# Two pairs of feed-forward units per layer as seven block products, with two of the four weight sums made by accumulating DMA

## What is computed

```
def swiglu(x, w_gate, w_up, w_down):
    return (jax.nn.silu(x @ w_gate) * (x @ w_up)) @ w_down
...
        x = x + 0.5 * swiglu(rms_norm(x, norm_g[i, 0]), ffn_w_gate[i, 0], ffn_w_up[i, 0], ffn_w_down[i, 0])
        h = rms_norm(x, norm_g[i, 1])
...
        x = x + mix @ w_o[i]
        x = x + 0.5 * swiglu(rms_norm(x, norm_g[i, 2]), ffn_w_gate[i, 1], ffn_w_up[i, 1], ffn_w_down[i, 1])
    return rms_norm(x, final_g)
```

## Time and profile before

| | |
|---|---|
| median of 3 runs | 1964.34 us (1964.17 to 1964.35) |
| the profiled execution | 1965.22 us, of it 1963.4 us span |
| PE busy | 1945.8 us (99%), 10556 matmuls |
| DVE busy | 1219.4 us (62%) |
| ACT busy | 949.7 us (48%) |
| POOL busy | 41.1 us (2%) |
| PE's share of the chain that ended last | 97% |
| DMA | 348.80 MB, 178 GB/s on average |
| granted PE clock | 0.996 of full speed |

### The profile page before, as it was taken

The page is one execution under the profiler, slowest core; times in us unless marked ns, Lnnn a source line. Parts: engine busy times, 40 slices in busy tenths (PEclk is TensorE's granted clock), DMA queues, the critical chain, the costliest instruction groups (busy, mean ns, idle before and its releaser), DMA issues.

```text
span 1963.4 us, 26311 instructions
## 1 busy us (share of the span) xinstructions
PE 1945.8 (99%) x10556; PEld 1681.9 (86%) x10556; DVE 1219.4 (62%) x1179; ACT 949.7 (48%) x1018; POOL 41.1 (2%) x34
## 2 busy tenths in 40 slices
PE   9999999999999999999999999999999999999998
PEld 7888998888888898888888889988888888988887
DVE  6555657655755678755575555775557556557554
ACT  5444545444544444644454443454445444545443
POOL 0000000000000000100000000000000000000000
PEclk9999999999999999999999999999999999999999
DMA  7654443555455453555445543445554554535541
GB/s 253 234 188 186 157 152 150 206 186 187 186 186 186 168 193 109 185 199 192 172 177 189 191 152 129 171 169 206 186 188 172 193 192 150 194 128 193 191 187 71
DMA packets 49872, 348.80 MB, mean 178 GB/s; under 512 B 6145, under 2 KB 6401, under 8 KB 7937
## 3 DMA queue, kind: packets, MB, share of 16 engines
q1 hardware_dynamic: 49360, 346.54, 47.9%
q10 hardware_dynamic: 432, 1.11, 0.2%
HBM read 346.58 MB, written 1.05 MB: 177 GB/s over the span
## 4 chain that ended last, share of the span: by engine, by line
PE 97%; DVE 2%; DMA 0%; ACT 0%; issue 0%; POOLq 0%; POOL 0%; DVEq 0%; ACTq 0%
PE work L1202 27%; PE work L1200 12%; PE acc L1071 9%; PE acc L1073 9%; PE acc L1072 9%; PE work L1071 7%; PE work L1073 7%; PE work L1072 7%; PE work L1205 2%; PE acc L1115 1%; PE work L1385 1%; DVE w_lo L629 1%; PE work L1372 1%; PE work L1262 0%; DMA x<-x_dram 0%; PE work L1386 0%
## 5 line engine op out<-in xcount | busy, mean ns | idle before, releaser
L629 DVE TENSOR_TENSOR w_lo<-raw,w_hi 128x2048 fp32r<-128x2048 f32 x327 | 746.7, 2288 | 123.7 <-ACT w_hi L376 121.2
L1202 PE MATMUL work<-xn,w_hi 128*128 128x512 f32 x2304 | 795.6, 393 | 0.0
L376 ACT ACTIVATE w_hi<-raw 128x2048 fp32r<-128x2048 f32 x327 | 620.9, 1908 | 16.0 <-DMA raw<-stream_dram 16.0
L1200 PE MATMUL work<-xn,w_lo 128*128 128x256 f32 x2016 | 567.4, 281 | 0.0
L1202 PEld LDWEIGHTS work<-xn,w_hi 128*128 128x128 f32 x2304 | 417.6, 188 | 75.6
L1200 PEld LDWEIGHTS work<-xn,w_lo 128*128 128x128 f32 x2016 | 379.7, 188 | 13.9
L1071 PE MATMUL acc<-w_hi,m_hi 128*128 128x512 f32 x824 | 325.1, 395 | 1.2 <-DVE m_lo L845 0.6
L1073 PE MATMUL acc<-w_hi,m_lo 128*128 128x512 f32 x824 | 321.2, 390 | 0.0
L1072 PE MATMUL acc<-w_lo,m_hi 128*128 128x512 f32 x824 | 320.8, 389 | 0.0
L435 ACT ACTIVATE scratch<-work 128x512 f32<-128x512 f32 x72 | 43.2, 600 | 431.9 <-PE work L1202 431.9
L726 DVE TENSOR_TENSOR scratch<-work,scratch 128x512 f32<-128x512 f32 x72 | 49.8, 692 | 276.3 <-ACT scratch L435 276.3
(11 more groups left out here) (177 smaller groups left out, 1721.9 us busy)
## 6 DMA issues: line engine op xcount, KB each, us to landing
raw<-stream_dram SPq DMA_DIRECT2D x327, 1024.0 KB, 4.8
x<-x_dram SPq DMA_DIRECT2D x2, 512.0 KB, 7.7
raw<-stream_dram ACTq DMA_DIRECT2D x2, 512.0 KB, 7.4
cst<-consts_dram SPq DMA_DIRECT2D x1, 832.0 KB, 6.8
out_dram<-x SPq DMA_DIRECT2D x3, 256.0 KB, 2.4
final_gain<-final_gain_dram SPq DMA_DIRECT2D x1, 512.0 KB, 7.5
out_dram<-wide SPq DMA_DIRECT2D x1, 256.0 KB, 2.9
cst<-consts_dram ACTq DMA_DIRECT2D x1, 64.0 KB, 1.9
```

The lines of the kernel that those rows point to most:

```text
L376: nc.scalar.activation(w_hi[:, c % RING, :], raw[:, c % RAW, :], ACT.Copy).then_inc(hi_ready, 1)
L629: nc.vector.tensor_tensor(w_lo[:, c % RING, :], raw[:, c % RAW, :], w_hi[:, c % RING, :].bitcast(F32), ALU.subtract).then_inc(lo_ready, 1)
L1200: nc.tensor.matmul(bank[:, 0:T], lo, xn_hi[:, k, :], start=False, stop=False, skip_group_check=True)
L1202: ins = nc.tensor.matmul(halves(bank), hi, xn[:, :, k, :], start=k == 0, stop=k == DT - 1, skip_group_check=True)
```

## The change

In each FFN the units 4 and 5, and the units 8 and 9, become a pair (`SEVEN = 4, 8`). The gate and up product of a pair is a matrix product of two token blocks (128 tokens each) by two halves of the inner dimension, with weights of two halves by two units: four blocks `b11`, `b12`, `b21`, `b22`, each a chunk of 512 inner rows by 512 columns (256 of gate, 256 of up). Eight block products would be needed; here seven are made (`PARTS`), from four sums of weight blocks (`t1` to `t4`) and four sums of token blocks (`S1` to `S4`):

- `t1` is `b11` plus `b12`, `t3` is `b12` plus `b22`: both sums are made by a DMA from POOL's queue that adds a second chunk from HBM onto a chunk in SBUF (`accum_op`). `b11` is loaded twice for that, the second time into a new buffer `extra`. The signs are in how the chunks are combined.
- `t2` is the sum of `t3` and `b11`, `t4` the sum of `b21` and `t2`: two adds on DVE of a whole chunk (`form`, L786 and L789), in place in `raw`, and in `extra`.
- each of the seven chunks is then split as any other; `quarter` makes one block product: 12 matmuls with tokens (or token sums) as stationary operand and 512 weight columns moving.
- the token sums are made once per FFN, in unit 2: four DVE adds, four ACT copies, four DVE subtractions of 512 numbers per partition (`token_sums`, `token_sums_hi`, `token_sums_lo`).
- the seven results are combined in PSUM, by accumulation, and on DVE and ACT (`pair_step`), and the hidden values are transposed on PE (`pair_hidden`: two groups of four transposes), during the gate of the unit after the pair.
- the down product of the unit after the first of a pair moves into the pair; the unit after the pair does two down products. The loops are gone; everything is written out in full. The weights are in the stream as loads (`LOADS`) and as uses (`USES`), which are no longer the same list: 376 uses, 344 loads and 32 adding DMAs, where before there were 328 of each.

The new order of chunks in units 7, 8, 9 and 10 is: top 7, bottom 7, down 6, then `b11`, `t1`, `t2`, `b21`, `t3`, down 7, `t4`, `b22`, then top 10, down 8, bottom 10, down 9, down 10. The diff, cut to its core:

```
+SEVEN = 4, 8
+PLAIN = [s for s in range(UNITS) if s not in SEVEN and s - 1 not in SEVEN]
+OWN = PLAIN[TURNED:]
+HIDDEN = [s for s in range(UNITS) if s not in OWN]
 PAIRS = D // COLS
-FFN_CHUNKS = 3 * UNITS
+FFN_CHUNKS = 3 * UNITS + 3 * len(SEVEN)
...
+def plan():
+    uses, loads, users, places = [], [], [], {}
+    for layer, n, c0, att, no in phases():
+        order = ATT_ORDER if att else FFN_ORDER
+        for w, (what, j) in enumerate(order, c0):
+            p = no * len(SEVEN) + SEVEN.index(j) if what in PARTS else None
+            if what in ("t1", "t4"):
+                uses.append((what, no, j, SUMS, None))
+            elif what == "b22":
+                uses.append((what, no, j, EXTRA, p + 1))
+            elif what in ("t2", "t3"):
+                uses.append((what, no, j, *places["b11" if what == "t2" else "b12"]))
+            else:
+                uses.append((what, no, j, len(users) % RAW, len(users) // RAW + 1))
+            for load in ("b12",) if what == "t1" else () if what in FORMS or what in ("t3", "b22") else (what,):
+                r = len(users)
+                places[load] = r % RAW, r // RAW + 1
+                loads.append((load, layer, n % 3, j, r % RAW, users[r - RAW] if r >= RAW else None))
+                users.append(("form", len(FORMS) * (p + 1)) if load in ("b11", "b21") else
+                             ("lo", c0 + order.index(("t3", j)) + 1) if load == "b12" else ("lo", w + 1))
+            if what == "t1":
+                earlier = SEVEN.index(j) - 1
+                loads.insert(-1, ("b11", layer, n % 3, j, SUMS,
+                              ("gu", (no * len(PLAIN) + TURNED) * TB) if earlier < 0 else
+                              ("lo", c0 + order.index(("t4", SEVEN[earlier])) + 1)))
+                loads.append(("b22", layer, n % 3, j, EXTRA,
+                              ("gu", (no * len(PLAIN) + TURNED) * TB) if earlier < 0 else
+                              ("lo", c0 + order.index(("b22", SEVEN[earlier])) + 1)))
+    return uses, loads
...
-                sp.dma_start(raw[:, c % RAW, :], stream[chunk]).then_inc(raw_loaded[c % RAW], 16)
+            def load(i):
+                place, free = LOADS[i][4:]
+                if free is not None:
+                    sp.wait_ge({"lo": lo_ready, "form": form_ready, "gu": gu_psum}[free[0]], free[1])
...
+
+                for i, j in enumerate(SEVEN):
+                    p = f * len(SEVEN) + i
...
+                    pool.wait_ge(sums_loaded, 16 * (p + 1))
+                    pool.dma_start(raw_at(SUMS), stream[b12], accum_op=ALU.add).then_inc(t1_ready, 16)
+                    pool.wait_ge(raw_loaded[place], 16 * loads_of_b12)
+                    pool.dma_start(raw_at(place), stream[b22], accum_op=ALU.add).then_inc(t3_ready, 16)
...
+                def own_step_of(s):
...
+                    if not after:
+                        split_to(g + 3)
+                    if s == TURNED:
+                        hidden_hi(s - 1, unit_bank(s - 1, 0))
+                    if ahead and not after:
+                        split_to(g + 5)
+                    act.wait_ge(top_used, plain + 1)
+                    nc.scalar.activation(gate_rest, own_bank(0)[:, :, T:2 * T], ACT.Copy).then_inc(gate_rest_ready, 1)
+                    split_to(g + (3 if after else 6 if ahead else 4))
+                    act.wait_ge(gate_ready, own_u + 1)
+                    nc.scalar.activation(gate_sb, gate_sb, ACT.Silu).then_inc(own_silu_ready, 1)
...
+                    if after:
+                        split_to(g + 6)
+                    act.wait_ge(gu_psum, plain * TB + 2)
+                    nc.scalar.activation(up_rest, own_bank(1)[:, :, T:2 * T], ACT.Copy).then_inc(up_rest_ready, 1)
+                    if not after:
+                        split_to(g + (7 if ahead else 5))
+                    act.wait_ge(own_h_ready, own_u + 1)
+                    nc.scalar.activation(m_hi[:, u % 2 * 2:u % 2 * 2 + 2, :], up_sb, ACT.Copy).then_inc(h_hi_ready, 1)
+                    if after:
+                        split_to(g + 7)
...
+                def pair_step(s):
...
+
+                    split_to(q + 5)
+                    copied(1, 0, first_part)
+                    split_to(q + 6)
...
+            def form(what, q):
+
+                no, j = USES[q][1:3]
+                p = no * len(SEVEN) + SEVEN.index(j)
+                place = {part: USES[q + PAIR_ORDER.index(part)][3] for part in PAIR_ORDER}
+                b11, b12, b21, b22 = (raw_at(place[part]) for part in ("t2", "t3", "b21", "b22"))
+                if what == "t2":
+                    dve.wait_ge(t3_ready, 16 * (p + 1))
+                    ins = nc.vector.tensor_tensor(b11, b12, b11, ALU.add)
+                else:
+                    dve.wait_ge(form_ready, len(FORMS) * p + 1)
+                    ins = nc.vector.tensor_tensor(raw_at(SUMS), b21, b11, ALU.add)
+                ins.then_inc(form_ready, 1)
 
...
+                def own_step_of(s):
...
+                    if not after:
+                        split_to(g + 3)
+                    if s == TURNED:
+                        hidden_lo(s - 1, unit_bank(s - 1, 0))
+                        token_sums()
+                    if ahead:
+                        split_to(g + 4)
+                        form("t2", g + 3)
+                        split_to(g + 5)
+                    dve.wait_ge(gate_rest_ready, own_u + 1)
                     nc.vector.tensor_tensor(gate_sb, own_bank(0)[:, :, 0:T], gate_rest, ALU.add).then_inc(gate_ready, 1)
-                    split_next(1)
-                    dve.wait_ge(up_rest_ready, own_u + 1 + turn * 2)
+                    split_to(g + (6 if after or ahead else 4))
+                    if ahead:
+                        form("t4", g + 3)
+                    dve.wait_ge(up_rest_ready, own_u + 1)
                     nc.vector.tensor_tensor(up_sb, own_bank(1)[:, :, 0:T], up_rest, ALU.add).then_inc(up_ready, 1)
-                    dve.wait_ge(own_silu_ready, own_u + 1 + turn * 2)
...
+                def quarter(bank, part, c, first, last):
+                    pe.wait_ge(lo_ready, c + 1)
+                    for k in range(FIRST_KS):
+                        a_hi, a_lo = part(k)
+                        ins = product(work[:, bank, :], a_hi, a_lo, wide_chunk(w_hi, c)[:, k, :], wide_chunk(w_lo, c)[:, k, :],
+                                      start=first and k == 0, stop=last and k == FIRST_KS - 1, skip=True)
+                    ins.then_inc(part_psum, 1)
+
+                def pair_step(s):
+                    p, q, own_u = f * len(SEVEN) + SEVEN.index(s), c0 + FFN_ORDER.index(("b11", s)), f * len(OWN) + OWN.index(s - 1)
+                    block_of = lambda tb, half: lambda k: tuple(
+                        w[:, half * FIRST_KS + k, tb * P:(tb + 1) * P] for w in (xn_hi, xn_lo))
+                    sum_of = lambda i: lambda k: token_part(i, k)
+                    pe.wait_ge(gate_ready, own_u + 1)
+                    quarter(0, block_of(0, 0), q, True, False)
+                    pe.wait_ge(up_ready, own_u + 1)
+                    if s == SEVEN[0]:
+                        pe.wait_ge(token_lo_ready, BANKS * (f + 1))
+                    quarter(3, sum_of(S1), q + 1, True, False)
+                    quarter(1, sum_of(S2), q + 2, True, False)
+                    pe.wait_ge(part_copied, 2 * p + 1)
+                    quarter(0, block_of(0, 1), q + 3, False, True)
+                    pe.wait_ge(pair_sums_ready, 5 * p + 1)
+                    quarter(1, sum_of(S3), q + 4, False, False)
+                    unit_down(s - 1).then_inc(down_used, 1)
+                    pe.wait_ge(pair_sums_ready, 5 * p + 2)
+                    quarter(1, block_of(1, 1), q + 6, False, True)
+                    pe.wait_ge(part_copied, 2 * p + 2)
+                    quarter(3, sum_of(S4), q + 7, False, True)
+
```

487 lines of the change are left out of this document (306 added, 181 removed).

## The result

The changed kernel takes 2101.16 us (median of 4 runs, 2099.76 to 2101.57) against 1964.34 us. The ratio is 1.069, with a 95% interval of 1.068 to 1.071. The direction was forecast, the size was not: +96 us was said, +137 came, and 2101 lies above the range's upper end of 2090.

What follows compares the result with a forecast made beforehand. PE was taken to bound the kernel, busy 1945.8 of 1963.4 us. Waits of 7.7 and 9.2 us less 4.9 gain give +12.0 per FFN, +96 in all: 2060 us, own range 2010 to 2090, with the other side 1933 to 2090.

Steps and rivals of the forecast that it cites:

- PE's gain, 39 us: PE's gate and up work with seven block products, less added transposes: 2.44 us won per pair, 39 us in all.
- The chain from `t3_ready` to `b21`, 19.1 us: Before each pair, serial DVE, ACT and load steps from the second add's end to PE's `b21`: 19.1 us.
- An add at twice the plain price, 4.98 us: Each adding DMA reads two chunks per one written, so it holds the DMA engines 4.98 us against 2.49.
- `t3_ready`: End of the second adding DMA, 14.9 us (pair 8) and 13.4 (pair 4) after the preceding unit's start; past 5.7 PE waits.
- The start of these transfers, -7.5: Before pair 8, the DMA engines are continuously busy from 7.5 us before unit 7 starts; `b11` goes out at -9.8.
- The sum, +12.0 per FFN: PE's waits of 7.7 us (pair 4) and 9.2 (pair 8) less the 4.9 gain, times 8: +96 us.
- The clock at nothing: Clock drops after PE's waits fall inside waits already counted: taken as 0, with 27 us kept for the upper end.
- Waits of PE over 130 us in all, by three causes: PE waits at `b11` for the gate add, `t1` for the up add, `b21` for ACT's copy: 7 to 10 us per pair.
- Rival adds at the plain price (1981): Adding DMAs cost as plain loads: +2.1 us per FFN, 1981 us; plain to 1.5 times the price, chance 0.20.
- Rival no hold-up (1935): Adds land 4.8 us after issue, no wait before pair 8: -3.6 us per FFN, 1935 us; chance 0.27.
- Its bound of 7.0 us for DVE before pair 4: DVE cannot form before 7.0 us after unit 3 starts, behind token subtractions and two splits; at least 1.3 us lost.
- Rival DVE as the bound: Each pair's DVE splits late by themselves, 1.3 us in both pairs: 1946 us; counted within the no hold-up case, no own chance.

Runs made afterwards that it cites:

- best_dve: Changed kernel with all four weight sums on DVE, the unit's own work before them, and combining adds ahead of splits: 1933.95 us, ratio 0.984 to the kernel before.
- second_only: Changed kernel with the first adding DMA of each pair left out, the second kept: 2025.93 us, ratio 1.031 to the kernel before.
- dma_alone: Only one-chunk DMAs, nothing of the kernel computed: SP's plain loads landed in 4.8 us, POOL's plain in 5.0, POOL's adding in 7.9.
- busy_waits: Changed kernel with 56 added PE products of zeros before each pair's wait for the gate add: 2105.16 us, ratio 1.071 to the kernel before.
- gate_first: Changed kernel with the gate add, copy and silu ahead of the split of `t1` and forming of `t2`: 2104.78 us, ratio 1.072 to the kernel before.
- best_dma_early: best_dma with the split of `t1` moved ahead of the copy and add of the up halves: 1994.58 us, ratio 1.016 to the kernel before.
- best_dma: Changed kernel, both adding DMAs kept, the unit's own work ahead of the sums, combining adds ahead of splits: 1978.12 us, ratio 1.007 to the kernel before.
- plain_copies: Changed kernel with both adding DMAs of each pair made plain copies of the same bytes: 2026.65 us, ratio 1.031 to the kernel before.
- no_adds: Changed kernel with both POOL DMAs of each pair left out: 1940.56 us, ratio 0.988 to the kernel before.
- one_add_early: one_add with the split of `t1` moved ahead of the copy and add of the up halves: 1943.71 us, ratio 0.990 to the kernel before.
- one_add: best_dma with `t1` formed on DVE, `b11` loaded once, only `t3` made by an adding DMA: 1970.57 us, ratio 1.003 to the kernel before.
- reorder: Changed kernel with DVE and ACT doing the unit's own gate, up and hidden work before forming `t2` and `t4`: 2036.53 us, ratio 1.037 to the kernel before.

## Why the prediction was right in direction and short in size

- **PE's gain, 39 us: right.** best_dve is 30.9 us faster, and its pairs are still 0.5 us late per FFN, 4 in all: 35 of 39. Where the last 4 us are was not found.
- **The chain from `t3_ready` to `b21`, 19.1 us: right.** 466.36 to 485.19 is 18.8.
- **An add at twice the plain price, 4.98 us: right** (5.0 alone, and second_only).
- **`t3_ready`: the step that failed.** 14.9 and 13.4 us were said; it was 17.1 before pair 8 and 15.1 before pair 4 in the second FFN. The prediction took the sum of the transfers, at the prices of the earlier trace rows, for the time of the landing. The windows of the changed kernel at that end (unit 7 starts at 449.30, so 14.9 is 464.2; the share of the DMA engines is the last number but one, and a packet counts whole in the window in which it starts):

```profile
462.00:464.00 2.00, 2.00 (x10) 1.65 (x10) 1.37 (x1) 0.60 (x1) 0.00 (x0) 1.00 1.01 213
464.00:466.00 2.00, 2.00 (x10) 1.38 (x8) 0.92 (x1) 0.00 (x0) 0.00 (x0) 1.00 0.37 74
465.00:466.00 1.00, 1.00 (x5) 0.56 (x3) 0.00 (x0) 0.00 (x0) 0.00 (x0) 1.00 0.05 8
466.00:468.00 2.00, 0.07 (x1) 0.00 (x0) 1.64 (x1) 0.00 (x0) 0.00 (x0) 1.00 0.00 0
```

  And the DMA queues in the 28.5 us from 438.5 to 467, in which the six loads from down 6 to `b21` and the two adds ran (packets, MB, share of the 16 engines):

```profile
q1 hardware_dynamic: 864, 6.29, 55.4%
q0 software_dynamic: 288, 2.10, 35.7%
```

  The loads took 15.8 us of the engines, 2.63 each and not 2.49, the adds 10.2 us, 5.09 each and not 4.98. For the five loads and two adds behind down 6 that is 0.9 us. Then, the 16 engines do not end together. By the packets and semaphore events of the trace, the parts of fifteen engines had landed at 465.53 and the last one's at 466.34; its last packet ended at 466.04, and DVE starts at 466.36. So, against 14.9: fifteen engines were through 1.0 us later, the last one 0.8 after them, and the landing came 0.3 after its last packet. In all sixteen pairs the last engine's part landed 0.3 to 1.2 us behind the fifteenth's.
- **The start of these transfers, -7.5: right by luck.** `b11` went out at 440.21, 9.1 before the unit and not 9.8. One reason is that both transpose groups fall into the top half of unit 6, which takes 6.46 us and not the 6.03 that were counted. And of the 2.3 us by which a lone load's landing exceeds its transfer (4.8 against 2.49), all of which the prediction put ahead of the transfer, only 1.0 lies there by the packets of dma_alone. What held `b11` was the load of down 6, whose last part landed at 442.62.
- **The sum, +12.0 per FFN, was +16.9.** Term by term: the sums' landing +1.9 and +2.2, from `b21` to the end of a pair +0.3 twice, for which the prediction had nothing, and 0.2 not placed. That is +4.9, or 39 us, of which 33 in the landings. The mechanism held. Of the +1.9 of pair 4, 0.4 are the first FFN's (12.7 late); how the other 1.5 divide was not worked out.
- **The clock at nothing: right here** (busy_waits). It holds where enough of the delay lies behind the slow stretch. In gate_first the wait is at `t1`, nearer to `b21`, and the slow matmuls behind it took up the 11 us that the shorter chain would have given. In best_dma_early the mean clock is 0.983 against 0.994 in best_dma, and part of its 16 us more may be the clock; that was not separated.
- **Waits of PE over 130 us in all, by three causes: nearly.** 123 us stand on the page, since the wait for the up add is hidden in the slow clock. The memory's figures were right (33.6 MB on POOL's queue, 396.9 MB from HBM), DVE's 1441 and ACT's 1047 us a little under the 1465 and 1060 said.
- **Rival adds at the plain price (1981): wrong as a number.** plain_copies gave 2027, as the chain over `t1_ready` takes over when `t3_ready` comes early, and the second copy was there at some 11.3 us and not 9.9. **Rival no hold-up (1935): right as a limit** (no_adds 1941). Its bound of 7.0 us for DVE before pair 4 should be 7.3 by its own terms (356.58, four times 0.69, two splits of 2.2), and it was not met either: in no_adds PE was 0.8 us late to `b21` there, not 1.3. **Rival DVE as the bound:** DVE at 78% in best_dve binds nothing.

## What to carry to other kernels

Before you move work to an idle engine, find where its result is used in the in-order lists: here a sum that was 1.5 us late for its own use (17.1, where `t2` needs it 6.5 before 22.1) made PE 11 us late, since the gate add, a split, a forming and a load stood behind it. Work out an arrival from the engine time queued before it, and add something for the slowest of the 16 DMA engines, which is the one that is waited for. And when several lists wait for a late thing, undo the order first and the lateness second: the order alone gave back 123 us (best_dma). Of the 44 us that best_dve has beyond that, one_add_early has 34 with one adding DMA still in each pair.

## What the runs showed of the hardware that was not expected

- An adding DMA of 1.049 MB into SBUF holds the DMA engines for 5.0 us against 2.49 for a plain load, and its fixed part is 2.9 us (dma_alone). The share of the engines reads 1.01 meanwhile, with only 213 GB/s from the adding ones, so a full share says nothing of the bytes.
- The 16 engines end their parts of a DMA at different times. The last one's part of the second add landed 0.3 to 1.2 us behind the fifteenth's in the changed kernel, and in one_add the latest add (9.1 us, median 8.0) was late by one engine alone: fifteen parts had landed 14.2 us after the unit's start, the last at 15.4.
- POOL's issue of an adding DMA took 0.86 us, and 1.21 for the second of two back to back; that of a plain one took 0.53 to 0.69.
- In reorder PE stood still for some 2.5 us before the unit after each pair. In ten of the sixteen pairs the granted clock was then at its lower level for a while, and that unit's gate took 8.1 us; in the other six it took 6.5.
